# Two MoE gathers in fp32r halves: the low part of the 64-token tile on the upper 64 partitions of its high part

## The reference

```python
def hier_moe(x, router_group_w, router_group_b, router_expert_w, router_expert_b, exp_w_gate, exp_w_up, exp_w_down):
    t = x.reshape(B * L, D)
    pg = jax.nn.softmax((t @ router_group_w + router_group_b).astype(f32), axis=-1)
    top_pg, grp = lax.top_k(pg, 1)
    ...
    top_le, ei = lax.top_k(le, TOP_K_INNER)
    w2 = jax.nn.softmax(top_le, axis=-1) * top_pg
    ...
    hid = jax.nn.silu(hg) * hu * gates[..., None].astype(hg.dtype)
    return jnp.einsum('tef,efd->td', hid, exp_w_down).reshape(B, L, D).astype(x.dtype)
```

## Time and profile before

| | |
|---|---|
| median of three runs | 1078.41 us |
| the profiled execution | 1070.39 us |
| its span | 1068.5 us |
| mean granted TensorE clock | 0.989 of full |
| TensorE busy | 1033.6 us (97%), 7349 products |
| VectorE busy | 815.6 us (76%) |
| ScalarE busy | 639.8 us (60%) |

### The profile page before, as it was taken

One profiled execution on the slowest core, in us unless ns is written; L12 is line 12 of the kernel. 1 busy time (PEld: TensorE's weight loads), 2 busy tenths in 40 slices (PEclk: granted clock), 3 DMA queues, 4 the chain that ended last, 5 costly groups with the idle time before them and its releaser, 6 DMA issues.

```text
span 1068.5 us, 17486 instructions
## 1 busy us (share of the span) xinstructions
PE 1033.6 (97%) x7349; PEld 871.5 (82%) x7349; DVE 815.6 (76%) x926; ACT 639.8 (60%) x660; POOL 19.0 (2%) x23
## 2 busy tenths in 40 slices
PE   9999999899999999999999999989999999999995
PEld 8899889877788888888878877677688888888884
DVE  7649545675788998999986677654878999998983
ACT  6556224524677767677755442445677777767664
POOL 0000000000000000000001300000000000000000
PEclk9999999999999999999999999989999999999998
DMA  9333000226399999999958779617199999999951
GB/s 373 132 115 107 21 4 3 73 80 248 133 343 347 368 362 360 362 362 369 354 221 349 296 281 376 257 41 275 53 353 324 375 351 355 357 365 366 372 212 52
DMA packets 40323, 271.04 MB, mean 254 GB/s; under 512 B 5057, under 2 KB 5521, under 8 KB 9521
## 3 DMA queue, kind: packets, MB, share of 16 engines
q1 hardware_dynamic: 39616, 267.11, 66.5%
q0 software_dynamic: 624, 2.76, 0.7%
HBM read 265.78 MB, written 4.07 MB: 253 GB/s over the span
## 4 chain that ended last, share of the span: by engine, by line
PE 84%; DVE 9%; ACT 3%; DMA 2%; issue 1%; ACTq 0%; SPq 0%; DVEq 0%
PE ps L925 11%; PE ps L927 11%; PE ps L926 11%; PE ps L959 5%; PE ps L961 5%; PE ps L960 5%; PE ps L352 3%; PE ps L354 3%; PE ps L353 3%; PE ps L1855 3%; DVE w_lo L346 2%; DMA raw<-in_stream 1%; PE ps L971 1%; PE ps L938 1%; PE ps L972 1%
## 5 line engine op out<-in xcount | busy, mean ns | idle before, releaser
L346 DVE TENSOR_TENSOR w_lo<-raw,w_hi 128x2048 fp32r<-128x2048 f32 x74 | 171.2, 2315 | 32.8 <-ACT w_hi L336 32.6
L336 ACT ACTIVATE w_hi<-raw 128x2048 fp32r<-128x2048 f32 x74 | 141.6, 1914 | 64.4 <-PE ps L927 25.8
L346 DVE TENSOR_TENSOR lo_more<-raw_more,hi_more 128x2048 fp32r<-128x2048 f32 x48 | 109.9, 2289 | 17.9 <-ACT hi_more L336 17.9
L346 DVE TENSOR_TENSOR lo_more<-raw,hi_more 128x2048 fp32r<-128x2048 f32 x48 | 109.9, 2290 | 11.9 <-ACT hi_more L336 11.9
L346 DVE TENSOR_TENSOR w_lo<-raw_more,w_hi 128x2048 fp32r<-128x2048 f32 x47 | 107.6, 2290 | 14.6 <-ACT w_hi L336 14.5
L336 ACT ACTIVATE hi_more<-raw 128x2048 fp32r<-128x2048 f32 x48 | 91.9, 1916 | 25.6 <-PE ps L927 25.6
L336 ACT ACTIVATE w_hi<-raw_more 128x2048 fp32r<-128x2048 f32 x47 | 90.1, 1917 | 16.2 <-PE ps L961 16.2
L336 ACT ACTIVATE hi_more<-raw_more 128x2048 fp32r<-128x2048 f32 x48 | 91.9, 1915 | 11.0 <-PE ps L961 9.6
L352 PE MATMUL ps<-h_hi,w_hi 128*128 128x320 f32 x272 | 87.1, 320 | 1.1 <-DVE arena L2579 1.1
L354 PE MATMUL ps<-h_hi,w_lo 128*128 128x320 f32 x272 | 84.6, 311 | 0.0
L353 PE MATMUL ps<-h_lo,w_hi 128*128 128x320 f32 x272 | 84.6, 311 | 0.0
(11 more groups left out here) (538 smaller groups left out, 2401.8 us busy)
## 6 DMA issues: line engine op xcount, KB each, us to landing
raw<-in_stream SPq DMA_DIRECT2D x125, 1024.0 KB, 6.8
raw_more<-in_stream SPq DMA_DIRECT2D x96, 1024.0 KB, 6.9
arena<-in_k_near SPq DMA_DIRECT2D x6, 1024.0 KB, 10.4
arena<-in_v_near SPq DMA_DIRECT2D x5, 1024.0 KB, 7.6
arena<-in_k_far SPq DMA_DIRECT2D x6, 512.0 KB, 8.7
kv_spare<-in_v_near SPq DMA_DIRECT2D x3, 1024.0 KB, 8.8
arena<-in_v_far SPq DMA_DIRECT2D x5, 512.0 KB, 6.8
kv_spare<-in_k_near SPq DMA_DIRECT2D x2, 1024.0 KB, 13.5
```

The source lines that it names most:

```text
L336: eng.activation(hi_slot(W_SLOT[c]), raw_chunk(c), ACT.Copy).then_inc(S("w_hi_made"), 1)
L346: eng.tensor_tensor(lo_slot(W_SLOT[c]), raw_chunk(c), hi_slot(W_SLOT[c]), ALU.subtract).then_inc(S("w_lo_made"), 1)
```

## The change

The low part of the third tile (64 tokens) no longer has a place of its own. It is written to partitions 64 to 127 of the same columns of `tok_hi`, whose partitions 0 to 63 hold the high part. The keys of the 64 tokens are made a second time for partitions 64 to 127, and `select_r` for the third tile has all 128 partitions, the upper half the same as the lower. One product of 128 rows then adds high and low part of the third tile, where there were two of 64 rows.

```diff
--- before.py
+++ after.py
@@ -699,11 +699,13 @@
 
         def token_low(eng, layer, n):
 
-            a, b = TOKEN_TILES[n % 3]
-            bank = HALF_BANKS[layer][0][n % 3]
+            bank, cols = HALF_BANKS[layer][0][n % 3], slice(512 * (n // 3), 512 * (n // 3) + 512)
             eng.wait_ge(S("tok_high"), 6 * layer + n + 1)
-            eng.tensor_tensor(tok_lo[n // 3][0:b - a, n % 3, :], ps[0:b - a, bank, :], tok_hi[0:b - a, n % 3, 512 * (n // 3):512 * (n // 3) + 512], ALU.subtract)\
-               .then_inc(S("tok_low"), 1)
+            if n % 3 == 2:
+                low, rows = tok_hi[64:P, 2, cols], slice(0, 64)
+            else:
+                low, rows = tok_lo[n // 3][:, n % 3, :], slice(0, P)
+            eng.tensor_tensor(low, ps[rows, bank, :], tok_hi[rows, n % 3, cols], ALU.subtract).then_inc(S("tok_low"), 1)
 
         def moe_dve(eng, layer, at):
             first, second = HALF_BANKS[layer]
@@ -734,13 +736,13 @@
             eng.wait_ge(S("placed"), layer + 1)
             keys = rb[:, :, 4:8]
             eng.tensor_tensor(keys[:, 0:2, :], hot[:, 0:2, :], ps[:, second[1], 0:8].rearrange("p (a b) -> p a b", a=2), ALU.mult)
-            eng.tensor_tensor(keys[0:64, 2, :], hot[0:64, 2, :], ps[0:64, second[1], 8:12], ALU.mult)
+            for rows in (slice(0, 64), slice(64, P)):
+                eng.tensor_tensor(keys[rows, 2, :], hot[0:64, 2, :], ps[0:64, second[1], 8:12], ALU.mult)
             next_reads(eng, eng.tensor_reduce(rs[:, 11, 0:1], ps[:, second[1], 12:16], AX, ALU.max))
             eng.tensor_scalar(flag, rs[:, 11, 0:1], float(P) + 0.5, None, ALU.is_lt).then_inc(S("flag_made"), 1)
-            for i, (a, b) in enumerate(TOKEN_TILES):
-                n = b - a
-                eng.tensor_tensor(select_r[0:n, i, :].rearrange("p (g s) -> p g s", g=4), places[0:n, :].unsqueeze(1).broadcast_to((n, 4, P)),
-                                  rb[0:n, i, 4:8].unsqueeze(2).broadcast_to((n, 4, P)), ALU.is_equal).then_inc(S("select_made"), 1)
+            for i in range(3):
+                eng.tensor_tensor(select_r[:, i, :].rearrange("p (g s) -> p g s", g=4), places.unsqueeze(1).broadcast_to((P, 4, P)),
+                                  rb[:, i, 4:8].unsqueeze(2).broadcast_to((P, 4, P)), ALU.is_equal).then_inc(S("select_made"), 1)
             eng.wait_ge(S("flag_made"), layer + 1)
             kept = steps[0]
             with eng.If(read_flag(eng, layer)):
@@ -966,12 +968,12 @@
             def gather():
 
                 def part(k, i):
-                    a, b = TOKEN_TILES[i]
                     cols = slice(P * k, P * k + P)
-                    eng.matmul(ps[:, k, :], tok_hi[0:b - a, i, cols], select_r[0:b - a, i, :], start=(i == 0), stop=False)
-                    mm = eng.matmul(ps[:, k, :], tok_lo[k // HT][0:b - a, i, P * (k % HT):P * (k % HT) + P], select_r[0:b - a, i, :], start=False, stop=(i == 2))
+                    mm = eng.matmul(ps[:, k, :], tok_hi[:, i, cols], select_r[:, i, :], start=(i == 0), stop=(i == 2))
                     if i == 2:
                         mm.then_inc(S("gathered"), 1)
+                    else:
+                        eng.matmul(ps[:, k, :], tok_lo[k // HT][:, i, P * (k % HT):P * (k % HT) + P], select_r[:, i, :], start=False, stop=False)
 
                 eng.wait_ge(S("tok_low"), 6 * layer + 6)
                 for i in range(3):
```

## The result

The changed kernel takes 1067.29 us, the median of nine runs (1066.22 to 1075.66); the kernel before takes 1075.99 us beside it, also in nine runs (1069.88 to 1080.96). The ratio is 0.9947 (95% interval 0.9925 to 0.997): faster by 0.53%, 5.7 us of 1076. The two medians lie further apart, 8.7 us, because nine executions that differ by 9 to 11 us among themselves do not fix a median; the ratio with its interval is the figure to use. The forecast gain was 5.8 us. The forecast time, 1072.6 us with a range of 1070.4 to 1075.6, was too high, for the most part because it was subtracted from a median of three runs that did not last.

What follows compares the result with a forecast made beforehand. TensorE was taken to bound the kernel. Its 3.76 us saved in the first layer, less 0.50 and 0.38, gave 2.88; 2 x 2.88 = 5.8 us off the 1078.41 median gave 1072.6 us, range 1070.4 to 1075.6.

Steps and rivals of the forecast that it cites:

- What bounds the kernel: Whole kernel: TensorE bounds it, busy 97% of the span, 84% of the chain; the gather is its own time.
- TensorE, 3.76 and 3.85 us: Gather, first and second layer: eight products and ten size changes fewer, 3.76 and 3.85 us less TensorE time.
- VectorE's delay, d = 0.50: VectorE ahead of the gather: flag 0.50 us later, from one instruction at 0.06 and four holds at 0.11.
- The wait for the gates: Before `place_rows`: TensorE newly waits for `gates_tok`, 0.38 us in the first layer.
- The gain of 2.88 us per layer: At `place_rows`: TensorE starts it 2.88 us earlier in each layer, after the later flag and the new gates wait.
- Rival 5: Clock halves at the new wait before `place_rows`, 3.4 us lost per layer, 1.1 us slower in all, 1079.5; chance 0.02.
- so I subtract from it: End of the sum: 5.8 us taken from the three runs' median 1078.41, not the profiled 1070.39, giving 1072.6 us.
- Rival 1: VectorE chain ahead of the gather not in the way or cheaper: 1071.8 us, or 1070.9 with gates hidden; chance 0.15.
- rival 4: Gather: two 64-row products share the array, so only size changes go, 1.42 us per layer, 1075.6; chance 0.03.
- Rivals 2 and 3: After the gather: VectorE's splits bound, 1075.0 us, chance 0.08; or loads set the pace, 1078.4 us, chance 0.04.
- nothing else is late: After the gather: splits keep 2.0 us of slack, ScalarE never waits for loads, so the shift carries to the end.

Runs made afterwards that it cites:

- nine_fillers: Changed kernel with nine filling products (results unread) instead of six before the gather; one execution, `hot` product to `place_rows` 13.55 and 13.29 us.
- again_before: The kernel before, run once more unchanged; ratio 0.9992 to the kernel before, median 1073.07 us.
- again_after: The changed kernel, run once more unchanged; ratio 0.9952 to the kernel before, median 1069.73 us.
- grouped: Kernel before with its last four tiles k ordered as the first four, leaving 4 of 10 size changes per gather; ratio 0.9961, median 1070.6 us.
- third_low_out: Kernel before without the products of the third token tile's low part; ratio 0.9962, median 1068.99 us.
- key_only: Kernel before with only the second key product, for partitions 64 to 127, added; one execution, 1078.48 us.
- upper_first: Changed kernel with the key product for the upper half first and the wide one last; ratio 0.9963 to the kernel before, median 1071.6 us.
- more_filler: Changed kernel with 14 filling products instead of six before the gather; ratio 0.993 to the kernel before, median 1067.57 us.
- one_filler_before: Kernel before with one filling product instead of six before the gather; one execution, `hot` product to `place_rows` 17.92 and 18.72 us.

## Why the prediction was right in its gain and wrong in its time

- **What bounds the kernel.** Right. From the second layer's first up product to the end of the span are 295.5 to 295.7 us in every trace, of either kernel and of the experiments: what is saved before it is carried to the end. The first layer's gain has to pass the stretch between the layers as well, and that I took for granted: it takes 463.8 to 465.9 us over all traces. Its wait for VectorE at L352, 0.96 us before and 1.23 after, is 1.49 in nine_fillers, but 0.35 in again_before and 0.16 in again_after. Whether a few tenths of the gain are lost there isn't shown. The sum as a whole holds: 5.5 us at equal clock, by the lines through the executions.
- **TensorE, 3.76 and 3.85 us.** Right. In the second layer the gather takes from 752.68 to its last product at 761.64, and with one start distance (0.23) 9.19 us, forecast 9.14; at full clock the first layer's takes 9.19 too (nine_fillers), forecast 9.27. Both terms were measured by themselves: 0.19 us a change was 0.20 to 0.21 (grouped), 1.84 us for eight products 1.9 (third_low_out).
- **VectorE's delay, d = 0.50.** Right, 0.49 and 0.51 us by the gather's start behind that of the filling products (2.93 against 2.44, 2.72 against 2.21), and its parts by key_only and upper_first.
- **The wait for the gates.** Right in kind, a little too small. The profile shows 0.40 us in both layers, but it counts from the modelled end of the last product. Counted as the forecast did, from the last start and one start distance more, TensorE stands 762.42 - (761.64 + 0.23) = 0.55 us in the second layer, forecast 763.03 - 762.56 = 0.47, and 0.56 in the first at full clock (nine_fillers), forecast 0.38. The chain moved as worked out, except that TensorE starts 0.14 us after the last gates instruction's end (762.07 + 0.21 against 762.42) and not 0.04, and that in the second layer `gathered_lo(0)` starts at 757.67, behind VectorE's own L780 and not only behind the bank.
- **The gain of 2.88 us per layer.** At full clock 2.77 (first layer, from more_filler) and 2.74 (second). The tenth that is missing is the 0.14 us, instead of 0.04, between the gates and TensorE's start.
- **Rival 5** came true in part, and at another place than I gave it. It was priced at the new wait of 0.4 us; what lowered the clock was the old wait before the gather, which d makes longer, 1.30 to 1.80 us. It cost 1.58 us in the first layer, not 3.4 in each, and left the sign as it was. The mechanism was named, its trigger wasn't: d was costed only as a delay, and not as idle time of TensorE.
- **The step that failed** is the last one of the sum, "so I subtract from it". The three runs' median lay 8 us above the profiled execution, and I took that as a property of the kernel that the change would keep. The runs showed that it was not: the same program's median was 1075.99 in nine runs and 1074.82 in 35, and its executions differ by the granted clock, in its two traces ahead of 230 us; those above 1078 us are the ones with the lowest clocks. (For the three runs themselves no clock is on record.) From 1074.82 the forecast gain gives 1069.0, and the changed kernel's twelve runs beside it had 1069.73. So of the 5.3 us between 1072.6 and the measured 1067.29, 3.6 are the starting value (1078.41 against 1074.82), 2.4 are that the first nine runs of the changed kernel came out low (1067.29 against 1069.73), and 0.7 go the other way, a gain of 5.1 by these medians where 5.8 was forecast. The range held this gain's uncertainty and hardly that of the starting value: 2.7 us, the spread of three runs, where nine runs spread over 11 us.

Rival 1 is out, d was 0.5 and the gates were met, and so is rival 4: the 64-row products, all on partitions 0 to 63, don't share the array. Rivals 2 and 3 are out as bounds, since no new wait for a split or a load came up in the first MoE and the time at equal clock fell by 5.5 us. The prediction's "nothing else is late" went too far, though. It looked at ScalarE's waits up to 560 us only, and the wait for a load that ends at about 586 us is there in every trace, 5.8 to 7.2 us long.

So of TensorE's 3.8 us in the first layer (13.03 - 9.19) 0.49 went to the later flag, 0.56 to the wait for the gates and what it takes to start behind it, and 1.58 to the lowered clock: 1.2 were left, and 2.74 in the second layer. These 3.9 us, and the 3.4 us by which the two spans differ, lie within the interval of the ratio, which is 3.2 to 8.1 us. The ratio's middle, 5.7, lies near to the forecast 5.8 in part by chance, since the forecast had no half clock in it.

## What to carry to other kernels

Before a gain is subtracted, ask where the runs and the profiled execution differ: a spread that comes from the granted clock ahead of the edit belongs to the execution, and a range needs it beside the terms of the sum. A delay of some tenths on one engine is also idle time on the one that waits for it; where that wait grows beyond what the trace has shown at full clock, fill it or price a clock drop. And before operands are packed together, count what order alone gives: keeping products of one shape together brought nearly half of the gain.

## What the hardware did that I had not expected

- TensorE's clock can halve after a wait of 1.57 to 2.02 us, and in other traces did not after 1.56 to 1.73: 3.3 us at 0.50 right behind it in the first gather, and in one_filler_before 4.7 us of products 0.43 us apart in the second. I had expected it at waits like the 4.4 us one alone. Eight more filling products take the loss away (more_filler), and so do three more (nine_fillers).
- One program's executions on one core differ by 10 us and more through stretches at half clock before 230 us, with TensorE busy for 219.0 to 219.6 of those 230 us in the four traces of the two kernels.
- A change between 128 and 64 rows costs a matmul stream 0.20 us, nearly a whole product of 512 columns; a 64-row product saves nothing over one of 128 (0.23 us both).
